# A fused transformer kernel: in the attention loop the first latent head pair and the first neighbourhood head pair exchange their places, and the output projection's pieces are dealt anew over the steps

## What is computed

```python
x = x + g1 * (jnp.concatenate([a_lat, b_lat, c_lat, d_lat], axis=-1) @ w_out[l])
# a: grouped-query attention, 4 heads of 64            ("g" in the kernel)
# b: 2-D neighbourhood attention, window 8 x 16, bias  ("n")
# c: differential attention, softmax(q1 k1) v - lam * softmax(q2 k2) v, RMSNorm   ("d", outputs "c")
# d: multi-head latent attention, q and k of 64 + 32   ("m")
# latents attend to their latent keys and all context keys in one softmax;
# the context (layer 0 only) attends to the context
```

## Time and profile before

| | us |
|---|---|
| median of 3 runs | 1527.97 |
| lowest, highest | 1526.56, 1530.21 |
| the profiled execution | 1533.84 |
| its span, first to last instruction | 1532.0 |
| TensorE busy in it | 1466.0 |
| mean granted TensorE clock, share of full speed | 0.993 |

### The profile page before, as it was taken

The page is one execution under the profiler, slowest core; times in us unless marked ns, Lnnn a source line. Parts: engine busy times, 40 slices in busy tenths (PEclk is TensorE's granted clock), DMA queues, the critical chain, the costliest instruction groups (busy, mean ns, idle before and its releaser), DMA issues.

```text
span 1532.0 us, 25197 instructions
## 1 busy us (share of the span) xinstructions
PE 1466.0 (96%) x9490; PEld 971.8 (63%) x9490; DVE 795.5 (52%) x1768; ACT 393.5 (26%) x895; POOL 306.1 (20%) x457
## 2 busy tenths in 40 slices
PE   5999999999999999999999999999999999999995
PEld 4655445766655558688888554556656667688883
DVE  2333533467676645655554753524667764743335
ACT  1322113345554520000000422113455541000001
POOL 0111101000000000365553121210000000354532
PEclk9999999999999999999999999999999999999998
DMA  9642112640011177699999754114811025589994
GB/s 353 209 165 110 56 42 90 217 156 15 29 42 42 42 265 287 249 322 368 354 359 338 284 179 142 65 56 131 264 54 42 15 104 201 200 307 339 339 359 170
DMA packets 104699, 282.01 MB, mean 184 GB/s; under 512 B 20037, under 2 KB 34157, under 8 KB 95097
## 3 DMA queue, kind: packets, MB, share of 16 engines
q1 hardware_dynamic: 91824, 259.52, 47.5%
q0 software_dynamic: 12192, 21.02, 3.7%
q10 hardware_dynamic: 584, 0.14, 0.0%
HBM read 259.44 MB, written 38.01 MB: 194 GB/s over the span
## 4 chain that ended last, share of the span: by engine, by line
PE 90%; DMA 3%; issue 2%; DVE 2%; ACT 1%; POOL 1%; SPq 0%; DVEq 0%; POOLq 0%; ACTq 0%
PE S L1346 19%; PE S L1742 17%; PE B L1525 9%; PE S L1753 8%; PE PT L1466 6%; PE B L1502 6%; PE S L1445 4%; PE B L1370 3%; PE B L1242 2%; DMA arena<-in_w_mod 2%; PE S L1370 2%; PE S L1435 2%; PE S L1423 1%; PE S L1609 1%; PE S L1616 1%
## 5 line engine op out<-in xcount | busy, mean ns | idle before, releaser
L1346 PE MATMUL S<-arena 128*128 128x512 f32 (+3 forms) x768 | 296.0, 535 | 2.6 <-ACT arena L1004 2.6
L1742 PEld LDWEIGHTS S<-arena 128*128 128x128 f32 x2240 | 257.5, 193 | 20.9 <-issue 20.9
L1742 PE MATMUL S<-arena 128*128 128x128 f32 x2240 | 258.7, 276 | 3.6 <-issue 3.5
L1346 PEld LDWEIGHTS S<-arena 128*128 128x128 f32 x768 | 139.8, 190 | 122.9 <-issue 102.1
L1114 ACT ACTIVATE arena<-S,nmax 128x768 f32<-128x768 f32 (+1 forms) x200 | 154.7, 778 | 149.4 <-DVE nmax L2260 79.3
L1920 POOL DMA_INDIRECT arena<-h,arena x140 | 150.3, 1074 | 163.1 <-DVEq L2558 103.8
L1525 PE MATMUL B<-arena 128*128 128x512 f32 x320 | 153.7, 602 | 0.6 <-DVE arena L2320 0.5
L1466 PEld LDWEIGHTS PT<-cst,arena 128*128 128x128 f32 x768 | 86.8, 141 | 71.1 <-issue 59.3
L1753 PE MATMUL S<-arena 128*128 128x512 f32 x280 | 126.0, 592 | 0.0
L1466 PE MATMUL PT<-cst,arena 128*128 128x128 f32 x768 | 114.4, 278 | 6.5 <-issue 4.8
L1502 PEld LDWEIGHTS B<-arena 128*64 128x64 f32 x1536 | 83.1, 136 | 37.4 <-issue 32.1
(11 more groups left out here) (332 smaller groups left out, 1753.9 us busy)
## 6 DMA issues: line engine op xcount, KB each, us to landing
arena<-in_w_mod SPq DMA_DIRECT2D x24, 2048.0 KB, 10.9
arena<-in_moe_w_gate SPq DMA_DIRECT2D x35, 1024.0 KB
arena<-in_moe_w_up SPq DMA_DIRECT2D x35, 1024.0 KB
arena<-in_moe_w_down SPq DMA_DIRECT2D x35, 1024.0 KB
arena<-in_w_in SPq DMA_DIRECT2D x6, 2048.0 KB, 11.1
arena<-y SPq DMA_DIRECT2D x20, 512.0 KB, 5.8
arena<-mod SPq DMA_DIRECT2D x16, 512.0 KB, 7.2
arena<-in_tokens SPq DMA_DIRECT2D x12, 512.0 KB, 9.8
```

The source lines that it names most:

```text
L1346: mm = pe.matmul(ubank[u % 4][:, c0:PANEL_W[p]], hT[:, k, t * P:(t + 1) * P], panel[p][:, k, c0:], start=k == 0, stop=k == KT - 1)
L1742: mm = pe.matmul(to, wgu[b][:, w, k * DE + h * P:k * DE + (h + 1) * P], XT[b][:, k, :], start=k == 0, stop=k == KT - 1)
```

## The change

STEPS puts m0 at step 3 and n0 at step 5, where n0 and m0 stood; JOBS follows, so that their `values` keep the distance of two steps; and PIECES is a new deal.

```diff
-STEPS = [("d", 0), ("g", 0), ("d", 1), ("n", 0), ("d", 2), ("m", 0), ("d", 3), ("n", 1), ("g", 1), ("m", 1)]
+STEPS = [("d", 0), ("g", 0), ("d", 1), ("m", 0), ("d", 2), ("n", 0), ("d", 3), ("n", 1), ("g", 1), ("m", 1)]
-JOBS = {3: ("g", 0), 4: ("c", 0), 5: ("n", 0), 7: ("m", 0), 8: ("c", 1), 9: ("n", 1), 10: ("g", 1), 11: ("m", 1)}
+JOBS = {3: ("g", 0), 4: ("c", 0), 5: ("m", 0), 7: ("n", 0), 8: ("c", 1), 9: ("n", 1), 10: ("g", 1), 11: ("m", 1)}
-PIECES = {0: (0, 2), 1: (2, 3), 2: (3, 5), 3: (5, 6), 4: (6, 8), 6: (8, 11), 7: (11, 12), 8: (12, 14), 9: (14, 16)}
+PIECES = {0: (0, 1), 1: (1, 3), 2: (3, 5), 3: (5, 7), 4: (7, 8), 5: (8, 9), 6: (9, 12), 7: (12, 14), 8: (14, 15), 9: (15, 16)}
```

## The result

| | before | after |
|---|---|---|
| median, us | 1527.97 | 1533.36 |
| lowest, highest | 1526.56, 1531.21 | 1530.11, 1536.3 |
| ratio, 95% interval | | 1.0030 (1.0019 to 1.0040) |
| the profiled execution, span | 1533.84, 1532.0 | 1531.44, 1529.6 |
| a tile 2 or 3 of layer 0 | 52.95 | 53.18 |

The forecast was 1528.4 us (range 1523.0 to 1533.0) and, likeliest, no difference. Measured twice more, on two chips and beside new runs of the kernel before, the changed kernel stood at 1.0017 (1.0006 to 1.0028) and 1.0016 (1.0000 to 1.0031). So by these ratios it is slower by 2.4 to 4.6 us where +0.4 was forecast, at the edge of what can be told from no change. The first median lies 0.4 us over the range; the forecast's base times the first ratio, 1527.97 x 1.0030 = 1532.6, lies inside.

A forecast was written before the change was run, and what follows sets the result against it. TensorE is busy 96%, so only its waits count: the 1.35 us saved returns in five small ones. Tile 0 +0.5 and -0.4, tiles 1 2 x 0.35, context -0.4: +0.4 on 1527.97, 1528.4 us (range 1523.0 to 1533.0).

The forecast's parts named there:

- the wait of 1.35: End of step 5: the scores of d3 wait 1.35 us for m0's second exponential; forecast to go.
- the slack that was forecast: Step 5 with n0 and one piece: TensorE's own work 4.31 us against a chain of 4.10, 0.2 to spare.
- The five new waits: Latent tile after the change, steps 6, 9, 0, 4 and 8: 0.17, 0.39, 0.38, 0.39 and 0.37 us lost.
- the old one of step 2: Second half of step 2's product waits for VectorE's copy of PT: 0.68 us in tiles 2 and 3 falls to 0.32.
- Context tiles: Tiles 4 and 5: the wait at step 6 goes, step 8 gives back 0.3; tile 5 gains 0.4 us, tile 4 nothing.
- Tile 0, layer 0: Last input block ends about 0.5 us later, and step 7's modulation load passes the whole shift on: +0.5 us.
- Tile 0, layer 1: Step 5 keeps 0.76 of the 1.35 us, -0.6; step 7's later load adds +0.2: -0.4, bounds -0.6 and +1.3.
- the upper bound: First tile of layer 1: +1.3 us, with step 7's modulation load issued up to 1.5 us later.
- A: One piece covers the copies: no waits in steps 4, 8, 9, 0 (1.53 us); gain 9.2 us, 1519.2; chance 0.13.
- B: VectorE's eviction ahead of n0 in step 5 starts past 0.5 us, delaying d3's scores: 4.2 us over forecast, 1532.6; chance 0.14.
- C: Many small waits lower TensorE's clock once a latent tile: about 1.5 us x 6 = 9 us, 1537.4; chance 0.03.

The follow-up runs named there:

- The exchange alone: m0 and n0 exchanged as in the change, but the pieces dealt as before, against the kernel before: ratio 0.9961 (0.9946 to 0.9976).
- the control: m0 and n0 exchanged, and from the old deal one piece moved from step 9 to step 5, against the kernel before: ratio 0.9971 (0.9957 to 0.9986).
- the kernel whose step 5 waits 3.4 us: m0 and n0 exchanged, one piece moved from step 4 to step 5 of the old deal, against the kernel before: ratio 1.0197 (1.0171 to 1.0222).
- the kernel with more cover: m0 and n0 exchanged, and from the old deal one piece moved from step 6 to step 5, against the kernel before: ratio 0.9969 (0.9957 to 0.9981).

## Why the prediction was right or wrong

**What bounds the kernel, and the wait of 1.35.** Right. It is gone, with the slack that was forecast.

**The five new waits, and the old one of step 2.** Right in place, and in size within 0.03 us each but for one term; where they miss, they are too small:

| step | forecast | measured |
|---|---|---|
| 6 | 0.17 | 0.20 |
| 9 | 0.39 | 0.40, and 0.08 at its head |
| 0 | 0.38 | 0.41 |
| 4 | 0.39 | 0.40 |
| 8 | 0.37 | 0.39 |
| 2 | 0.32 | 0.32 |
| sum | 2.02 | 2.20 |

The 0.08 is a term that the prediction did not have: in step 9 the scores follow the small product by 0.29 (411.80 to 412.09), by 0.21 before (411.50 to 411.71), where that product had not waited. A further 0.06 is spread over the joints. Together 0.24 a tile: tile 2 came to +0.23 where 0.0 was forecast, tile 1 to +0.59 where +0.35 was, over six latent tiles 1.4 us.

**Context tiles.** The large wait went as forecast (steps 3 to 7 of tile 5: 15.87 before, two more pieces at 0.86, less 0.69, makes 16.90; measured 16.89). Step 8 and step 9 are 0.08 longer each. Tile 4: +0.18 for 0.0; tile 5: -0.24 for -0.4. Another 0.34 us.

**Tile 0, layer 0.** This step failed, without harm. The load for step 7 is the second of the two in the earlier trace rows: the first is issued behind the modulation product of step 4, the second behind the last input block. In a timeline that keeps the two apart the second is issued here before and after:

```profile
284.82 0.54 SPq L669 DMA_DIRECT2D arena<-in_w_mod  x1
```

```profile
284.63 0.54 SPq L669 DMA_DIRECT2D arena<-in_w_mod  x1
```

The tile starts at 236.90 before and at 236.27 after. So the issue is later by 0.44 us (47.92 to 48.36 from the start of the tile), as the forecast of 0.5 had it. But "so the whole shift goes through" is wrong: the product that waits for the load starts 59.06, 59.09 and 58.86 us after the start of the tile in the three traces of the changed kernel, and 59.41 and 59.08 in the two of the kernel before.

```profile
295.33 3.46 PE L1242 MATMUL B<-arena,cs 128*32 128x128 f32 x64 [2.17 <-DMA arena<-in_w_mod]
```

From issue to product it takes 10.70, 10.73 and 10.50 us in those three traces and 11.49 and 11.15 in those two; the two runs of the old order with another deal or with the cut copy give 11.53 and 9.69. The load's own time varies by more than the shift. What sets it, no experiment was made for.

**Tile 0, layer 1.** The tile takes 66.11 us in the second trace of the kernel before and 65.44 in the first of the changed one: steps 0 to 8 gained 0.67, forecast -0.4 with bounds of -0.6 and +1.3. (The first trace of the kernel before has 67.22 there: groups of matmuls that are whole elsewhere stand broken off in the middle, once for 0.49 us inside a modulation product, with nothing in the profile that they wait for.) But the load for step 9 can then come too late. Second run of the changed kernel:

```profile
1097.28 1.95 PE L1242 MATMUL B<-arena,cs 128*32 128x128 f32 x64 [0.73 <-DMA arena<-in_w_mod]
```

Such a wait of 0.6 to 1.0 us stands there in nine of the ten profiled executions with the exchange, and in none of the four in the old order; the tile takes 66.25 and 66.35 us in the two traces of the changed kernel that have it. The load is issued at almost the same time in both orders, 47.52 us into the tile before and 47.62 after. In the changed kernel the product that waited for it started 15.83 and 15.93 us behind the issue; in the kernel before it came after 16.00 and 15.79 and found the load there. So the old order had next to no time to spare at this load, and what the steps ahead of it gain turns into a wait, unless the load is as quick as in the first trace of the changed kernel, where the product started 15.02 behind the issue without one. That is like the mishap that the upper bound allowed for, at the next load and at a smaller size.

**The sum.** By steps, where +0.4 was forecast: about 0 for tile 0 of layer 0 (75.69, 75.72 and 75.53 us after, 75.93 and 75.08 before, so it can be a few tenths either way), +0.59 +0.23 +0.23 for its tiles 1 to 3, +0.18 and -0.24 for the context, between -0.67 and +0.24 for tile 0 of layer 1, +0.60 +0.23 +0.23 for the others: 1.4 to 2.3 us, against 2.5 us by the second and third measurement, whose intervals hold it. The first measurement's 4.6 (its interval starts at 2.9) is not explained by steps; nothing between the two layers' attention loops was found that differs, and whether about 1 us more is lost stays open. The forecast came as close as it did with some luck: its latent tiles came out 1.4 us too short and its context tiles 0.3, and the 0.5 us that it added for tile 0 of layer 0 and that didn't come took a part of that away.

**The rivals.** A (the copies are covered) is refuted by the waits in the table and by the cut of the copy, which won from the waits that A denied. B did not happen in the changed kernel (0.41 us against a limit of 0.5), but a piece moved by one step made its mechanism cost 2%. C did not happen: the granted clock is 1.00 in all six latent tiles of each of the three traces after.

**Where the gain went.** The exchange alone is worth 6 us by its ratio (3.7 to 8.3 by the interval), of which the latent tiles show 3.7. The deal that came with it takes pieces from between the halves of products, where each covered 0.4 us of VectorE's copy, and puts them, but for the one in step 5, where they cover nothing.

## What to carry to other kernels

Count filler work twice: it costs its own time wherever it stands, and it is worth the wait that it covers; moving it pays only if it covers more at its new place. Two edits don't add up when both claim the same wait, or when one makes longer what the other uncovers, so price each alone and then the second with the first in place. Before a piece of work is moved, look for whoever needs the last of a group (here the eviction at the head of another engine's step): one piece in the wrong step cost more than all the waits of a tile together. And when a copy between two halves is what limits them, it can be cut as well as covered: either took about 1 us off a tile here (1.0 for the cut, 0.9 to 1.3 for the deal of the control), and the two together took 1.5 to 1.8.

## What the runs showed of the hardware

**The clock after a wait is not the same each time.** In the kernel whose step 5 waits 3.4 us, step 6 of tile 1 ran at 0.72 of full speed and took 6.20 us, while step 6 of tile 2, after a wait of 3.3, ran at 1.00 and took 4.56; in tile 1 of layer 1 it was 0.61 and 7.35. 1.00 is 2.4 GHz; the others are means of stretches at 2.4 and at 1.2 GHz. Read in windows of 1 us from 346.20 on, the clock is 0.86, 0.50 (the last row), 0.50, 0.50, 0.94 and 1.00, so it fell after TensorE had started again:

```profile
346.20:352.40 6.20, 6.20 (x24) 3.22 (x24) 4.26 (x9) 2.52 (x5) 0.00 (x0) 0.72 0.00 0
403.29:407.85 4.56, 4.56 (x23) 2.37 (x23) 3.39 (x8) 2.52 (x5) 0.00 (x0) 1.00 0.00 0
1150.10:1157.45 7.35, 7.35 (x24) 3.58 (x24) 4.27 (x9) 2.52 (x5) 0.00 (x0) 0.61 0.00 0
347.20:348.20 1.00, 1.00 (x6) 1.00 (x6) 0.94 (x2) 0.00 (x0) 0.00 (x0) 0.50 0.00 0
```

The modulation product of step 7, layer 0, shows the same over executions. After a wait of 2.17 us it took 3.46 (above); after one of 2.57, in the kernel with more cover, the granted clock stayed at 1.00 and it took 1.95. Of the thirteen traces with such a wait (1.97 to 2.57 us) four had the full clock in the 2 us behind it (after waits of 2.10 to 2.57) and nine 0.50 to 0.70 (after 1.97 to 2.48):

```profile
295.72 1.95 PE L1242 MATMUL B<-arena,cs 128*32 128x128 f32 x64 [2.57 <-DMA arena<-in_w_mod]
```

**A faster product can gain nothing there.** In that execution the next modulation product, in step 9, waited 1.40 us for its load and started 73.15 us after the start of the tile; where the first had taken 3.46, it started after 72.89. It does not always come to nothing: of the two traces of the kernel before, the one with the full clock there (2.11 for the product) took 75.08 us for the tile, the other (3.46) 75.93.

**A cut copy is cheap.** 512 and 256 columns took 0.68 and 0.41, and 1.00 from the start of the first to the end of the second (376.92 to 377.92), against 0.95 for 768 columns in one.
